# Hyena / mLSTM diffusion step: residual, output product, down products and final norm from feature-major to token-major

## The reference

```python
h = _rmsnorm(x, norm_mix_w) * (1 + scale_m) + shift_m
proj = h @ w_in                      # -> Hyena | mLSTM, each 512 features of y
x = x + gate_m * (concatenate([y_hy, y_ml]) @ w_out)
h = _rmsnorm(x, norm_ffn_w) * (1 + scale_f) + shift_f
up = dwconv3x3(h @ ffn_w_up) ; a, val = split(up)        # 2 x 2816 columns
x = x + gate_f * ((silu(a) * val) @ ffn_w_down)
y = _rmsnorm(x, final_norm_w)
```

## Time and profile before

| | us |
|---|---|
| median of 3 runs | 1636.09 |
| lowest, highest | 1632.84, 1636.24 |
| span of the profiled execution | 1634.9 |
| TensorE busy (matmuls) | 1557.1, 95% |
| DVE, ACT, POOL busy | 982.4 (60%), 490.3 (30%), 473.0 (29%) |

### The profile page before, as it was taken

How to read it: one execution, slowest core, us unless ns; L and a number is a source line. 1 busy time by engine, 2 the same in 40 slices (tenths; PEclk the granted TensorE clock), 3 DMA queues, 4 the chain that set the end, 5 groups by cost and what they waited for, 6 DMA issues and landing times.

```text
span 1634.9 us, 22924 instructions
## 1 busy us (share of the span) xinstructions
PE 1557.1 (95%) x9583; PEld 1434.9 (88%) x9583; DVE 982.4 (60%) x1368; ACT 490.3 (30%) x698; POOL 473.0 (29%) x213
## 2 busy tenths in 40 slices
PE   5889999999899798999899999999999999999996
PEld 1477899999899798999799999999999999999995
DVE  5656134787225347424888638855882786388835
ACT  2574123222432356434423102211221122022203
POOL 1665113111311187054322213222232222132210
PEclk9899999999999999999999999999999999999998
DMA  9753423433545695500111011110110111101102
GB/s 349 291 203 132 159 70 131 170 125 132 175 129 192 194 317 183 168 26 26 41 38 50 28 52 39 40 52 26 52 52 26 52 40 38 52 32 47 52 13 116
DMA packets 111193, 168.10 MB, mean 103 GB/s; under 512 B 6379, under 2 KB 88435, under 8 KB 105971
## 3 DMA queue, kind: packets, MB, share of 16 engines
q1 hardware_dynamic: 109039, 164.24, 29.0%
q10 hardware_dynamic: 2052, 2.40, 0.4%
HBM read 135.35 MB, written 31.27 MB: 102 GB/s over the span
## 4 chain that ended last, share of the span: by engine, by line
PE 56%; DVE 3%; ACT 1%; issue 0%; POOL 0%; ACTq 0%; DVEq 0%
PE psum L231 18%; PE psum L233 18%; PE psum L235 18%; DVE mlp_acc_a L3128 1%; DVE tail_scan_h L3008 1%; PE psum L3232 0%; PE psum L3392 0%; DVE mlp_h_lo L3014 0%; DVE w_raw L3197 0%; DVE mlp_h_lo L3002 0%; DVE mlp_acc_a L3197 0%; DVE tail_x L3152 0%; DVE mlp_h_lo L3059 0%; ACT tail_x L2905 0%; PE psum L3263 0%
## 5 line engine op out<-in xcount | busy, mean ns | idle before, releaser
L231 PE MATMUL psum<-mlp_h_hi,w_hi 128*128 128x384 f32 (+2 forms) x1248 | 305.1, 340 | 6.2 <-DVE mlp_acc_a L3128 3.5
L233 PE MATMUL psum<-mlp_h_lo,w_hi 128*128 128x384 f32 (+2 forms) x1248 | 301.4, 337 | 0.0
L235 PE MATMUL psum<-mlp_h_hi,w_lo 128*128 128x384 f32 (+2 forms) x1248 | 300.9, 336 | 0.0
L3128 DVE SCALAR_TENSOR_TENSOR w_raw<-psum,par,w_raw 128x945 f32<-128x945 f32 (+2 forms) x176 | 214.7, 1220 | 91.6 <-ACT w_raw L2949 87.9
L3128 DVE SCALAR_TENSOR_TENSOR mlp_acc_a<-psum,par,mlp_acc_a 128x945 f32<-128x945 f32 (+2 forms) x176 | 214.5, 1219 | 33.1 <-ACT mlp_acc_a L2949 29.9
L2720 POOL TENSOR_TENSOR w_lo<-w_raw,w_hi 128x2048 fp32r<-128x2048 f32 x32 | 148.2, 4630 | 288.3 <-ACT w_hi L2714 288.3
L231 PEld LDWEIGHTS psum<-mlp_h_hi,w_hi 128*128 128x128 f32 x1248 | 205.7, 189 | 25.3 <-issue 6.3
L233 PEld LDWEIGHTS psum<-mlp_h_lo,w_hi 128*128 128x128 f32 x1248 | 206.4, 189 | 15.3
L235 PEld LDWEIGHTS psum<-mlp_h_hi,w_lo 128*128 128x128 f32 x1248 | 206.2, 189 | 15.3
L3152 DVE SCALAR_TENSOR_TENSOR tail_x<-psum,mod,tail_x 128x384 f32<-128x384 f32 (+1 forms) x192 | 94.8, 515 | 128.3 <-PE psum L235 128.1
L231 PE MATMUL psum<-tail_g_hi,w_hi 128*128 128x384 f32 x480 | 160.3, 334 | 0.0
(11 more groups left out here) (383 smaller groups left out, 2499.6 us busy)
## 6 DMA issues: line engine op xcount, KB each, us to landing
w_raw<-ffn_w_up SPq DMA_DIRECT2D x22, 1024.0 KB, 4.9
filt_ada<-ada_w SPq DMA_DIRECT2D x16, 1024.0 KB, 9.2
w_raw<-w_in SPq DMA_DIRECT2D x13, 1024.0 KB, 5.7
w_raw<-ffn_w_down SPq DMA_DIRECT2D x11, 1024.0 KB, 4.9
scan_rows_spread<-scratch_scan_rows SPq DMA_DIRECT2D x18, 512.0 KB, 5.5
rownorm_ada<-ada_w SPq DMA_DIRECT2D x8, 1024.0 KB, 6.5
rownorm_x<-x_sample SPq DMA_DIRECT2D x8, 512.0 KB, 5.3
scratch_kt<-kt_spec SPq DMA_DIRECT2D x4, 1024.0 KB, 3.8
```

What stands on the lines that cost most here:

```text
L231: ins = nc.tensor.matmul(out, wh, x_hi(k, i), start=begin, stop=False)
L233: ins = nc.tensor.matmul(out, wh, x_lo(k, i), start=False, stop=False)
L235: ins = nc.tensor.matmul(out, wl, x_hi(k, i), start=False, stop=end)
L3128: ins = stt(out=out, in0=image(up_at)[:, r0 + dy:r1 + dy, c0 + dx:c1 + dx], scalar=weight(i, loc, t), in1=out, op0=ALU.mult, op1=ALU.add)
```

## The change

x is held token-major, tile t as a row of 1024 per token (`x_tile`), loaded straight into place. In the output, down and last products the activations (y, the gated product) are the stationary operand, 128 tokens at a time, and rows of w_out and w_down move, 512 wide. The 18 output half tiles use six banks. The gate now lies along the row: it is written to DRAM element by element in the projection (`store_gates`), and read back spread over all partitions (`load_gates`). DVE multiplies a product in PSUM by the gate row into a two-place buffer, and GpSimd adds that to x; for the last tile DVE adds too. The RMS norm before the FFN is made per token row (ACT Square with its sum, root, DVE reciprocal, ACT scaling), and the scaled rows are transposed (`norm_chunk`), after which one DVE operation from PSUM makes gain and shift. The final norm reads and writes x in place. The reserved DMA scratch is made smaller (4096).

```diff
+            def store_gates(which):
+                if which:
+                    sp.wait_ge(ada_mod, 1)
+                for j in range(2):
+                    src = mem["mod"][:, 16 + 24 * which:24 + 24 * which, j:j + 1]
+                    sp.dma_start(dram["gate_rows"][which, j].rearrange("(b p o) -> p b o", p=P, o=1), src, allow_slow_non_contiguous=True).then_inc(gates_out, 16)
...
+                if n in (18, 19):
+                    store_gates(n - 18)
...
+            def load_gates(which):
+                src = dram["gate_rows"][which:which + 1].rearrange("o j d -> o (j d)").broadcast_to([P, 2 * D])
+                sp.dma_start(gate_rows[:].rearrange("p j d -> p (j d)"), src).then_inc(gate_in, 16)
...
+            for i, t in enumerate(order):
+                last = (D * i + D - 1) // T
+                sp.wait_ge(hy_lo, min(last + 1, HC))
+                if last == HC:
+                    sp.wait_ge(gated_ml, NT)
+                sp.dma_start(x_tile(t), io["x_sample"][0, t * P:(t + 1) * P, :] if t < 8 else io["x_prompt"][0]).then_inc(x_in[t], 16)
+                if i == HC - 1:
                     sp.wait_ge(c_copied, 3)
                     sp.dma_start(io["new_C"][0, 0].rearrange("d h e k -> e (d h) k"), c_out).then_inc(state_out, 16)
                     sp.dma_start(io["new_n"][0, 0].rearrange("d h k -> (d h) k"), n_out).then_inc(state_out, 16)
...
+            def out_add(m):
+                t, half = out_tile(m), m // NT
+                pool.wait_ge(out_scaled, m + 1)
+                pool.wait_ge(x_in[t], 16)
+                at_ = half_of(x_tile(t), half)
+                nc.gpsimd.tensor_tensor(at_, at_, scaled_product[:, m % 2, :], ALU.add).then_inc(x_added, 1)
...
+            for m in range(NT):
+                out_add(m)
+            split_lo(pool, 0)
+            for t in range(4):
+                out_add(NT + t)
+            chunk_lo(range(4))
+            out_add(NT + 4)
+            chunk_lo(range(4, KD))
+            for t in range(5, 8):
+                out_add(NT + t)
...
+            def down_add(m):
+                half, t = down_place(m)
+                pool.wait_ge(down_scaled, m + 1)
+                at_ = half_of(x_tile(t), half)
+                nc.gpsimd.tensor_tensor(at_, at_, scaled_product[:, m % 2, :], ALU.add).then_inc(added, 1)
...
+                        for n in range(NT):
+                            down_add(m + n)
+                        split_lo(pool, unit("d", pair, half) + 2)
...
+            m = TILES * (PAIRS - 1)
+            for n in range(8):
+                down_add(m + n)
             gated_lo(LAST, 1)
+            down_add(m + 8)
...
+            for t in range(NT - 1):
+                pool.wait_ge(last_scaled, t + 1)
+                nc.gpsimd.tensor_tensor(x_tile(t), x_tile(t), last_rows[t % 2], ALU.add).then_inc(last_added, 1)
...
+            def row_root_of(t):
+                act.wait_ge(x_added, NT + t + 1)
+                if t == 0:
+                    act.wait_ge(out_lo, 2)
+                    act.wait_ge(eps_set, 1)
+                else:
+                    act.wait_ge(row_summed, t)
+                nc.scalar.activation(square, x_tile(t), ACT.Square, accum_out=row_sq[:, t:t + 1]).then_inc(row_summed, 1)
+                act.wait_ge(row_summed, t + 1)
+                nc.scalar.activation(row_root[:, t:t + 1], row_sq[:, t:t + 1], ACT.Sqrt, scale=1.0 / D, bias=eps[:]).then_inc(row_roots, 1)
+            def scale_row(t):
+                act.wait_ge(row_rstds, t + 1)
+                if t >= 4:
+                    act.wait_ge(norm_turned, KD if t < 7 else 2 * KD)
+                nc.scalar.activation(normed[t % 4], x_tile(t), ACT.Copy, scale=row_rstd[:, t:t + 1]).then_inc(row_normed, 1)
...
+            for t in range(NT - 1):
+                act.wait_ge(last_added, t + 1)
                 if t:
                     act.wait_ge(summed, t)
                 else:
                     act.wait_ge(gated, 2 * STEPS)
-                nc.scalar.activation(halves(final_square), tile_banks(t), ACT.Square, accum_out=sum_sq[:, t:t + 1]).then_inc(summed, 1)
-                act.wait_ge(means, t + 1)
-                nc.scalar.activation(root[:, t:t + 1], mean_sq[:, t:t + 1], ACT.Sqrt).then_inc(roots, 1)
+                nc.scalar.activation(square, x_tile(t), ACT.Square, accum_out=sum_sq[:, t:t + 1]).then_inc(summed, 1)
...
+            def scale_out(m):
+                t, half = out_tile(m), m // NT
+                dve.wait_ge(full, m + 1)
+                if m == 0:
+                    dve.wait_ge(gate_in, 16)
+                if m >= 2:
+                    dve.wait_ge(x_added, m - 1)
+                tt(scaled_product[:, m % 2, :], ps[:, m % 6, :], half_of(gate_rows[:, condition(t), :], half), ALU.mult)\
...
+                    ins = nc.vector.tensor_scalar(place(n)[:, a:z], ps[:, 6 + n % 2, a:z], mem["gain_ffn"][:, k, j:j + 1],
+                                                  mem["mod"][:, 24 + k, j:j + 1], ALU.mult, ALU.add)
...
-            def down_add(m):
-                cb, b = down_place(m)
+            def scale_down(m):
+                half, t = down_place(m)
                 dve.wait_ge(down_done, m + 1)
-                src, gate = ps[:, 6 + m % 2, :], mem["mod"][:, 40 + cb, :]
-                parts = ((0, BW, 0),) if b < 2 else ((0, BW - LP, 0), (BW - LP, BW, 1))
-                for a, z, j in parts:
-                    out = x[:, cb, BW * b + a:BW * b + z]
-                    ins = stt(out=out, in0=src[:, a:z], scalar=gate[:, j:j + 1], in1=out, op0=ALU.mult, op1=ALU.add)
...
+            def scale_last(t):
+                if t == 0:
+                    dve.wait_ge(g_lo_done, 2 * STEPS)
+                if t >= 2:
+                    dve.wait_ge(last_added, t - 1)
+                dve.wait_ge(last_done, 2 * t + 2)
+                tt(halves(last_rows[t % 2]), last_banks(t), halves(gate_rows[:, condition(t), :]), ALU.mult).then_inc(last_scaled, 1)
...
+            def finish(t):
                 dve.wait_ge(roots, t + 1)
...
+                stt(out=x_tile(t), in0=x_tile(t), scalar=rstd[:, t:t + 1], in1=norm_w, op0=ALU.mult, op1=ALU.mult).then_inc(scaled, 1)
...
+            for t in range(NT - 1):
+                scale_last(t)
+                if t >= 2:
+                    finish(t - 2)
+            t = NT - 1
+            for half in range(2):
+                dve.wait_ge(last_done, 2 * t + half + 1)
+                if half == 0:
+                    dve.wait_ge(last_added, t - 1)
+                row, at_ = half_of(last_rows[t % 2], half), half_of(x_tile(t), half)
+                tt(row, last_banks(t)[:, half, :], half_of(gate_rows[:, condition(t), :], half), ALU.mult).then_inc(last_scaled, 1)
+                dve.wait_ge(last_scaled, t + half + 1)
+                if half == 0:
+                    dve.wait_ge(added, FIRST)
+                    dve.wait_ge(last_added, t)
+                tt(at_, at_, row, ALU.add).then_inc(last_added, 1)
+                finish(NT - 3 + half)
+            dve.wait_ge(summed, NT + 1)
+            tt(sum_sq[:, t:t + 1], sum_sq[:, t:t + 1], sum_sq[:, t + 1:t + 2], ALU.add).then_inc(joined, 1)
+            finish(t)
...
+            def out_part(m, ks):
+                wh, wl = (late_hi, late_lo) if m >= NT else (w_hi, w_lo)
+                a = P * out_tile(m)
+                if m >= 6 and ks[0] == 0:
+                    pe.wait_ge(out_scaled, m - 5)
+                for k in ks:
+                    if m < NT and k == HC:
+                        pe.wait_ge(ml_lo, m + 1)
+                if m == NT and ks[0] == 0:
+                    pe.wait_ge(out_lo, 2)
+                ins = product(nc, [ps[:, m % 6, :].rearrange("p (u c) -> p u c", u=2)],
+                              lambda k: y_hi[:, k, a:a + P], lambda k: y_lo[:, k, a:a + P],
+                              lambda k, _: wh[:, :, 256 * k:256 * k + 256], lambda k, _: wl[:, :, 256 * k:256 * k + 256],
+                              ks, first=ks[0] == 0, last=ks[-1] == KD - 1)
+                if ks[-1] == KD - 1:
...
+                pe.wait_ge(row_normed, tiles_of(p).stop)
+                for i, t in enumerate(tiles_of(p)):
+                    ins = nc.tensor.transpose(ps[:, 6 + n % 2, i * P:(i + 1) * P], normed[t % 4][:, k * P:(k + 1) * P], mem["ident"][:])
+                ins.then_inc(norm_turned, 1)
...
+            def down_tile(m, wh, wl, gh, gl):
+                _, t = down_place(m)
+                a = P * t
                 if m >= 2:
-                    pe.wait_ge(added, m - 1)
-                product(nc, [ps[:, 6 + m % 2, 0:BW]], lambda k: wh[:, k, c:c + P], lambda k: wl[:, k, c:c + P],
...
+            for m in range(6, NT + 4):
+                out_part(m, range(KD))
+            for t in (4, 5):
+                for i in range(4):
+                    out_part(NT + t, range(2 * i, 2 * i + 2))
+                    norm_chunk(4 * (t - 4) + i)
+            for t in (6, 7):
```

(100 more changed lines are left out.)

567 lines of the change are left out of this document (204 added, 363 removed).

## The result

The change makes the kernel slower: 1641.37 us as the median of 6 runs (1639.63 to 1644.97) against 1636.53 of the kernel before in its 6, a ratio of 1.0034 with a 95% interval of 1.0023 to 1.0045. The forecast was 1627, faster. The profiled execution spans 1639.7 us, 4.8 more than that of before.

The account below looks back on a forecast made before the run. TensorE, busy 95% of the span, was taken as the bound. Output stage -8.7, down products -3.9 and tail +3.7 gave -8.9 us on 1634.9, so 1626.0, and 1627 us as median; range 1614 to 1638.

Parts of the forecast that it names:

- bounds of 0 and 5: Projection: the four gate stores delay transfers TensorE waits for by nothing at least, 5 us at most; 0 taken.
- Even at half of the row's time the four are through before 434.66: Projection: reason for taking 0; gate stores priced by the 5.7 us row of a 1024 KB w_in load.
- among the rivals, at 6%: Projection: gate stores make the y loads land late, +5 us, total 1632; chance 0.06.
- The rate: Down products: 216 matmuls of 512 columns at 0.227 us, 49.0 us a pair of steps against 49.9.
- Just hidden: Down adds: the 4.63 us weight split between adds 8 and 9 costs nothing, except 0.5 us in the last pair.
- forecast of -3.9: Down products: five pairs save 4.4 us by wider matmuls, less 0.5 us lost in the last pair.
- three waits of 0.8, 0.8 and 2.9 us: Output stage: TensorE waits for normed rows before transposing pieces 0, 1 and 2.
- my rival: Output stage: longer norm waits cost 6 us, clock drops 7.8 us in all; total 1641, chance 0.14.
- -8.7: Output stage, first product to first centre tap: 141.1 us falls to 132.4, new waits and slow clock included.
- Forecast +3.7: Tail: GpSimd's add and DVE's norm_w multiply exclude each other, cycle 4.86 us a tile, 3.7 us lost.
- Tail unhindered: Tail: GpSimd and DVE interleave or DVE gets in first; 41.8 us, 7.7 saved, total 1616, chance 0.16.
- the norm chain: Output stage rival: transposes waiting for normed rows stop TensorE; 1641, chance 0.14; two thirds into it set the range's top.

Follow-up runs that it names:

- before_stores: The kernel before with only the four gate stores of 1024 single elements added in the projection; 1642.03 us, ratio 1.0039.
- down_split: Changed kernel with the FFN gate's two stores moved to the output stage, plus GpSimd's weight splits behind the fourth and eleventh adds; 1628.93 us, ratio 0.9955.
- tail_dve: Changed kernel with the adds of the tail's first eight tiles on DVE instead of GpSimd; 1633.09 us, ratio 0.9981.
- tail_psum: Changed kernel with the FFN gate's two stores moved to the output stage, plus ACT scaling tail rows into PSUM for DVE's multiply; 1623.47 us, ratio 0.9926.

## Why the prediction was wrong

**Gate rows: the step that turned the sign.** I took 0 from bounds of 0 and 5; it is 7.0 in the changed kernel, 5.7 by before_stores. "Even at half of the row's time the four are through before 434.66" was a guess at a price that no row showed, chosen by bytes, and the four were not through. From the windows, a pair keeps the DMA engines busy for some 8 us (424 to 431, again 434 to 442), about 4 us a store as an estimate, where half of the row's time is 2.85. The upper bound was also short: it counted how long the stores themselves trail (to about 441, which is what the windows show) and not that the w_in load of 1 MB stands between them and the loads that TensorE waits for. The mechanism was among the rivals, at 6%; it deserved more, because there TensorE had no slack at all. That the same price is free in a gap of the queue and dear behind it (two stores nothing, four 6 to 7 us) I had not seen.

**Down products: half right.** The rate was right: 216 matmuls at 0.227 take 49.0 us in down_split where a pair took 49.9 before. The step that failed is "Just hidden": I looked at the split between adds 8 and 9 and not at the one ahead of add 0. The timeline of POOL after, first pair:

```profile
916.94 4.61 POOL L2700 TENSOR_TENSOR w_lo<-w_raw,w_hi 128x2048 fp32r<-128x2048 f32 x1 [11.81 <-ACT w_hi L2694]
921.51 3.79 POOL L2807 TENSOR_TENSOR tail_x<-tail_x,mlp_scaled_product 128x512 f32<-128x512 f32 x3
```

and of DVE:

```profile
915.46 0.69 DVE L3118 TENSOR_TENSOR mlp_scaled_product<-psum,mlp_gate_rows 128x512 f32<-128x512 f32 x1 [0.21 <-PE psum L235]
...
918.78 1.19 DVE L3094 SCALAR_TENSOR_TENSOR mlp_acc_a<-psum,par,mlp_acc_a 128x945 f32<-128x945 f32 x1
922.90 0.69 DVE L3118 TENSOR_TENSOR mlp_scaled_product<-psum,mlp_gate_rows 128x512 f32<-128x512 f32 x1 [2.93 <-POOL tail_x L2807]
```

The split starts late, when ACT's rounding behind a SiLU lets it, and runs exactly when the first product is ready to be added. The third multiply waits 2.93 us, and TensorE loses 0.38 us in each of the first four pairs (49.38 us a pair); the last, where the gated product's split stands there too, loses 2.4 (51.43). The five pairs together are 249.6 us before, 248.9 after and 245.0 in down_split: 4.6 us to be had, 3.9 of them lost in waits that I had at 0.5. The median of down_split is lower by the same 3.9. The stretch of the table has -1.1 for a forecast of -3.9; what it has beyond the pairs' -0.7 is within its spread.

**Output stage: the waits right, the clock not.** I had three waits of 0.8, 0.8 and 2.9 us; they are 0.77, 0.77 and 2.83. Too small was the clock, in two terms. At the start the granted clock is 0.52 (663 to 667 us), and nine matmuls of 512 take 4.0 us where at full clock they need 2.0, the transposes behind them 0.35 more: 2.4, not 1.4. Behind the wait of 2.83 the granted clock falls:

```profile
786.00:790.00 4.00, 4.00 (x17) 3.42 (x17) 3.15 (x9) 1.67 (x4) 0.73 (x1) 0.57 0.02 4
```

0.57 for 4 us is 1.7 us lost, which stood in my rival and not in the forecast, though the same rows priced it. With the waits' handovers (0.35) and 0.8 us spread over the stage this makes the 3.9 us between -8.7 and -4.8.

**The tail: right.** Forecast +3.7 with a multiply of 3.6 us, found +2.5 with 3.4 and the cycle 4.69. The mechanism was the one forecast. The cause is shown from both sides, GpSimd taken away (tail_dve) and the operand moved out of SBUF (tail_psum). "Tail unhindered" was 41.8 us for this stretch; tail_psum has 41.6.

**Sum.** The forecast missed by 13.7 us of the span: 6.9 of gate stores, 3.9 of the output stage, 2.8 of the stretch with the down products, 1.3 of a late start that no edit explains, less 1.2 of the tail. The gate stores alone are half of it. (The range had a slip of its own: two thirds of the way into the norm chain is 1636, not 1638.) The three pieces of the mechanism that I had to find in the old trace were found; the error is that small costs with a cover were each put at nothing.

## What to carry over

A transfer that joins a queue is priced by its number of pieces and by what stands behind it (here four stores of 1024 elements, 4 KB each), above all ahead of a place where the bound engine already waits; move it to where the queue is idle before anything else. When work goes from one instruction (multiply and add from PSUM) to a pair on two engines with a small buffer, go through the second engine's list for every long instruction ahead of and between its new ones, not only in the middle. And a pair of engines that shuts each other out is cured by an operand in PSUM, not only by moving the work.
